# Two conditioning blocks moved late into the first mixer, chunk 9's second token tile made in chunk 10, and fewer unread products

## Chip, cores and metric

One core of one Trainium2 chip runs the kernel. The metric is the device time of one execution in microseconds (us); the median of 3 runs of the kernel before is 1123.04 us (1118.69 to 1125.08).

## What is computed

Two layers over x of 256 tokens by 1024 features. Each layer is three post-normalised sub-layers: a SwiGLU FFN, a block of four token mixers side by side, and a second SwiGLU FFN. Every sub-layer has its own shift, scale and gate, made from one conditioning vector c. Cut to what matters here:

```python
cs = jax.nn.silu(c)
for l in range(DEPTH):                      # 2
    mod = (cs @ ada_w[l] + ada_b[l]).reshape(bn, 3, 3, D_MODEL)
    shift, scale, gate = mod[:, :, 0, None], mod[:, :, 1, None], mod[:, :, 2, None]
    u = x * (1.0 + scale[:, 0]) + shift[:, 0]
    y = _swiglu(u, ffn_w13[l, 0], ffn_w2[l, 0])          # (silu(a) * g) @ w2, D_FF = 2816
    x = _layer_norm(ALPHA * x + 0.5 * gate[:, 0] * y, ln_g[l, 0], ln_b[l, 0])
    u = x * (1.0 + scale[:, 1]) + shift[:, 1]
    y = _hybrid_mixer(u, ...)     # window attention, top-k attention, mLSTM, S5 + GLU, then w_out
    x = _layer_norm(ALPHA * x + gate[:, 1] * y, ln_g[l, 1], ln_b[l, 1])
    u = x * (1.0 + scale[:, 2]) + shift[:, 2]
    y = _swiglu(u, ffn_w13[l, 1], ffn_w2[l, 1])
    x = _layer_norm(ALPHA * x + 0.5 * gate[:, 2] * y, ln_g[l, 2], ln_b[l, 2])
```

## The kernel before, in words

Five engines each run one written-out order of instructions, tied by semaphores. There is no planner: what an engine does next is what stands next in its block.

**FFN.** D_FF is cut into 11 chunks of 256 columns (`CHUNKS`), c = 0 to 10. TensorE (`ffn_chunk`, lines 571 to 618) makes for a chunk the 96 in-products of 256 columns: two tiles `ft`, two halves, eight slices of features, and three products each, because every f32 operand is split into a high and a low fp32r part. Then it makes 24 out-products of 512 columns, in four parts of six: token tile `tt` (0 or 1) by `ft` (0 or 1). They add into banks 0 to 3 of PSUM over all chunks. Tile tt ends in banks 2tt and 2tt+1. In the last chunk the parts come in the order (tt, ft) = (0,0), (0,1), (1,0), (1,1) and each bank raises `y_ready`. ScalarE makes silu (line 1712) and the high parts of the weights (`w_in_high` 1719, `w_out_high` 1727). VectorE multiplies by the gate half and splits h into parts (`ffn_tile`, 1073 to 1083), and makes the low parts of the weights (`w_in_low` 1088, `w_out_low` 1093).

**The conditioning.** `ada_w` is summed on VectorE in blocks of 512 columns: eight multiply-adds of 128x512 for one block (`ada_block`, lines 1007 to 1025) from a 2 MB load. Nearly all blocks stand at the end of an FFN chunk. Block 10 is loaded in two halves into `xn` and `rot_flat` and is summed in chunk 10 of layer 0's first FFN, four steps ahead of each `ffn_tile` (lines 1335 to 1338). Block 11 is loaded into `work_flat` and summed at the start of layer 0's mixer, between the residual and `s5_rotate_in(0)` (line 1428). Both are read only after the mixer, by `ada_sum(10)` and `ada_sum(11)`.

**The sub-layers' ends.** `deepnorm` (1110 to 1168) on VectorE takes banks 0 and 1 (`gated`, `with_x`, `statistics` for both halves, then the variance), then banks 2 and 3 in the same way; after the mixer alone (s == 1) the second tile is done half by half. ScalarE normalises, TensorE turns xn (`turn`, 505 to 520), and ScalarE and VectorE make the next u from it (`evac_uT`). Between these TensorE runs `ada_sum` products and products that nobody reads (`keep_busy`, line 525).

**The mixer.** VectorE's order late in it: logits of A up to `sink_arg` (line 1535); a wait for `g_spread`; the arguments w (1541, 1542); the convolution's last product (1547), after which TensorE can make line 870; scans; line 1559; rotations out, `s5_skip` (1568), `gelu_argument` (1574), `gelu_product` (1580); the products for oT (1633, then 1637 which raises `od_ready`); then `w_in_low` twice for FFN 2 and `deepnorm`. TensorE needs `od_ready` for the third of the four products of bank 0 in line 920.

**The load queue.** SyncE issues every load, in one order, and waits in that order for the buffers. Late in the mixer the order is: the pieces of w_in; `load_last_out` (453); `load_ffn_in` for chunk 0 of FFN 2 (341), which waits for `w_in_used` of the slot that the mixer's piece 4 reads, raised by `chunk_done(4)` (716) on TensorE; then waits for `cols_turned`, `g_spread` and `conv_step`; `load_ln` (356); `load_ffn_out` (349).

## Time and profile before

| | us |
|---|---|
| median of 3 runs | 1123.04 |
| the profiled execution, its own time | 1119.33 |
| its span in the profile | 1117.0 |
| TensorE busy | 1050.7 (94% of the span) |
| VectorE busy | 906.1 (81%) |
| ScalarE busy | 423.3 (38%) |
| mean granted TensorE clock | 0.984 of full speed |

Stages of the profiled span, by the first products of each: FFN 1 of layer 0 from about 35 to 237 us, its mixer to 374, FFN 2 to 573, FFN 1 of layer 1 to 776, its mixer to 906, FFN 2 to 1103. A timeline row reads: start, length, engine, line, operation, output from inputs, shapes, count; in brackets the idle time of the engine before it and what ended it. Matmuls are pipelined, so the length of one is more than its distance to the next.

### The profile page before, as it was taken

The numbers are of one execution on the slowest core, as the hardware profiler recorded it, in microseconds if no ns is written. First come the engines' busy times: TensorE is split into PE (matmuls) and PEld (weight loads), VectorE is DVE, ScalarE is ACT, GpSimd is POOL, SyncE is SP. The second block draws the span as 40 slices with busy tenths as digits, with TensorE's granted clock in tenths as the row PEclk, the third lists the DMA queues.
The fourth block names the chain that finished last, engine by engine and source line by source line (L and its number), as shares of the span: only waits on it lengthen the run. The fifth ranks groups of instructions, "written<-read, shape, count | busy, mean of one in ns | idle before, by whom it ended". The sixth has DMA issues, their size and how long they took to land.

```text
span 1117.0 us, 17050 instructions
## 1 busy us (share of the span) xinstructions
PE 1050.7 (94%) x6899; PEld 916.8 (82%) x6899; DVE 906.1 (81%) x1523; ACT 423.3 (38%) x574; POOL 35.0 (3%) x56
## 2 busy tenths in 40 slices
PE   1899999988999999999999999999999999999994
PEld 1899989976875789999989989998787568999994
DVE  6798999988975898988879998698897588755555
ACT  0445334322372343333333453332336244333331
POOL 1000000003000000000000000000300000000000
PEclk9899999998999999999999999999999999999998
DMA  9889998972351578898965886787225157564540
GB/s 369 283 307 329 345 306 292 323 219 76 94 190 38 189 267 298 304 320 309 328 211 188 303 290 215 269 313 201 108 86 205 50 187 244 174 225 148 193 151 38
DMA packets 184505, 250.84 MB, mean 225 GB/s; under 512 B 25372, under 2 KB 133216, under 8 KB 183404
## 3 DMA queue, kind: packets, MB, share of 16 engines
q1 hardware_dynamic: 184428, 249.76, 65.7%
q8 instruction: 55, 0.90, 0.3%
q14 instruction: 22, 0.18, 0.0%
HBM read 248.69 MB, written 1.05 MB: 224 GB/s over the span
## 4 chain that ended last, share of the span: by engine, by line
PE 73%; DVE 16%; DMA 4%; issue 3%; ACT 3%; SPq 1%; POOL 0%; POOLq 0%; DVEq 0%; ACTq 0%
PE PS L587 11%; PE PS L588 11%; PE PS L586 11%; PE PS L695 8%; PE PS L610 5%; PE PS L614 5%; PE PS L613 5%; DMA w_in_ring<-in_ffn_w_dram 4%; DVE w_in_lo L1088 3%; PE PS L920 2%; PE PS L702 2%; DVE acc L1024 2%; PE PS L780 2%; ACT w_in_hi L1719 2%; PE PS L561 2%
## 5 line engine op out<-in xcount | busy, mean ns | idle before, releaser
L588 PE MATMUL PS<-u_hi,w_in_lo 128*128 128x256 f32 x1280 | 359.9, 281 | 0.0
L587 PE MATMUL PS<-u_lo,w_in_hi 128*128 128x256 f32 x1280 | 359.1, 281 | 0.0
L586 PE MATMUL PS<-u_hi,w_in_hi 128*128 128x256 f32 x1280 | 358.8, 280 | 0.0
L586 PEld LDWEIGHTS PS<-u_hi,w_in_hi 128*128 128x128 f32 x1280 | 241.7, 189 | 1.8
L587 PEld LDWEIGHTS PS<-u_lo,w_in_hi 128*128 128x128 f32 x1280 | 240.4, 188 | 1.6
L588 PEld LDWEIGHTS PS<-u_hi,w_in_lo 128*128 128x128 f32 x1280 | 240.2, 188 | 0.0
L1088 DVE TENSOR_TENSOR w_in_lo<-w_in_ring,w_in_hi 128x2048 fp32r<-128x2048 f32 x88 | 201.2, 2289 | 30.4 <-ACT w_in_hi L1719 30.3
L1719 ACT ACTIVATE w_in_hi<-w_in_ring 128x2048 fp32r<-128x2048 f32 x88 | 168.0, 1914 | 4.1 <-DMA w_in_ring<-in_ffn_w_dram 4.1
L610 PE MATMUL PS<-w_out_hi,h_parts 128*128 128x512 f32 x352 | 145.0, 412 | 11.3 <-DVE h_parts L1082 11.3
L1727 ACT ACTIVATE w_out_hi<-w_out_ring 128x1024 fp32r<-128x1024 f32 x88 | 88.6, 1055 | 152.8 <-PE PS L614 152.8
L1712 ACT ACTIVATE arena<-PS 128x256 f32<-128x256 f32 x88 | 33.8, 384 | 286.5 <-PE PS L588 263.8
L614 PE MATMUL PS<-w_out_hi,h_parts 128*128 128x512 f32 x352 | 138.3, 393 | 0.0
L613 PE MATMUL PS<-w_out_lo,h_parts 128*128 128x512 f32 x352 | 138.1, 392 | 0.0
L1093 DVE TENSOR_TENSOR w_out_lo<-w_out_ring,w_out_hi 128x1024 fp32r<-128x1024 f32 x88 | 103.6, 1219 | 16.3 <-ACT w_out_hi L1727 16.0
L1024 DVE SCALAR_TENSOR_TENSOR acc<-arena,cs,acc 128x512 f32<-128x512 f32 x126 | 94.7, 752 | 4.5
L695 PE MATMUL PS<-uT,w_in_ring 128*128 128x256 f32 (+1 forms) x416 | 96.1, 388 | 1.3 <-issue 1.0
L610 PEld LDWEIGHTS PS<-w_out_hi,h_parts 128*128 128x128 f32 x352 | 66.1, 188 | 33.6 <-issue 20.9
L695 PEld LDWEIGHTS PS<-uT,w_in_ring 128*128 128x128 f32 (+1 forms) x416 | 78.1, 191 | 17.1 <-issue 5.6
L1077 DVE TENSOR_TENSOR arena<-arena,PS 128x256 f32<-128x256 f32 x88 | 36.7, 417 | 68.1 <-ACT arena L1712 67.9
L614 PEld LDWEIGHTS PS<-w_out_hi,h_parts 128*128 128x128 f32 x352 | 66.1, 188 | 15.7
L613 PEld LDWEIGHTS PS<-w_out_lo,h_parts 128*128 128x128 f32 x352 | 66.1, 188 | 15.4 <-issue 2.6
L1082 DVE TENSOR_TENSOR h_parts<-arena,h_parts 128x256 fp32r<-128x256 f32 x88 | 37.4, 425 | 3.0
(305 smaller groups left out, 1183.3 us busy)
## 6 DMA issues: line engine op xcount, KB each, us to landing
w_in_ring<-in_ffn_w_dram SPq DMA_DIRECT2D x88, 1024.0 KB, 7.7
arena<-in_ada_w_dram SPq DMA_DIRECT2D x30, 2048.0 KB, 8.4
w_out_ring<-in_ffn_w_dram SPq DMA_DIRECT2D x44, 1024.0 KB, 6.2
w_in_ring<-in_w_in_dram SPq DMA_DIRECT2D x6, 1024.0 KB, 7.2
w_in_ring<-in_w_in_dram SPq DMA_DIRECT2D x10, 512.0 KB, 5.2
w_out_ring<-in_w_out_dram SPq DMA_DIRECT2D x4, 1024.0 KB, 10.1
w_in_ring<-in_w_in_dram SPq DMA_DIRECT2D x2, 2048.0 KB, 8.7
w_in_ring<-in_w_out_dram SPq DMA_DIRECT2D x4, 1024.0 KB, 5.9
```

The costliest lines, as they stand in the source:

```text
L586: pe.matmul(y, hi, u_hi[:, kt, :], start=(i == 0), stop=False)
L587: pe.matmul(y, hi, u_lo[:, kt, :], start=False, stop=False)
L588: mm = pe.matmul(y, lo[:, kt, half, :], u_hi[:, kt, :], start=False, stop=(i == KT - 1))
L610: mm = pe.matmul(y, h_hi, w_out_hi[ft][:, cols], start=(first and ft == 0), stop=False)
L613: pe.matmul(y, h_hi, w_out_lo[slot][:, ft, cols], start=False, stop=False)
L614: mm = pe.matmul(y, h_lo, w_out_hi[ft][:, cols], start=False, stop=(last and ft == 1))
L695: mm = pe.matmul(o[0:w, :], w_in_ring[(G_MIX + m) % 2][:, kt, c0:c0 + w], uT[:, kt, :], start=(i == 0), stop=(i == KT - 1))
L1024: v.scalar_tensor_tensor(acc[:, :], part(buf, t), cs[:, t:t + 1], acc[:, :], ALU.mult, ALU.add).then_inc(sem("acc_step"), 1)
L1088: v.tensor_tensor(w_in_tile(w_in_lo, slot, ft), w_in_tile(w_in_ring, slot, ft), w_in_hi[ft][:, :, :, :].bitcast(F32), ALU.subtract).then_i ...
L1093: v.tensor_tensor(w_out_lo[slot][:, ft, :], w_out_ring[slot][:, ft, :], w_out_hi[ft][:, :].bitcast(F32), ALU.subtract).then_inc(sem("w_out ...
L1719: a.activation(w_in_hi[ft][:, :, :, :], w_in_tile(w_in_ring, slot, ft), ACT.Copy).then_inc(sem("w_in_high"), 1)
L1727: a.activation(w_out_hi[ft][:, :], w_out_ring[slot][:, ft, :], ACT.Copy).then_inc(sem("w_out_high"), 1)
```

## The change

On VectorE, blocks 10 and 11 are summed as eight pairs of two steps each: pairs 0 to 3 are block 10, pairs 4 to 7 block 11. Each pair has a load of 512 KB, into four buffers used twice (half of `uT_lo`, the two rows of `ln_bc`, half of `rot_flat`). Pairs 0 and 1 stand right after `sink_arg`, pair 2 after `gelu_argument(0)`, 3 after `s5_skip(1)`, 4 and 5 after `gelu_product(1)`, 6 after the oc products, 7 after the od products. From pair 2 on a load waits for the sum of the pair two before it. For layer 0 one `w_in_low` is moved from before the deepnorm after the mixer to after `evac_uT`, and at the end of FFN 2 another is moved in the same way.

In chunk 10 the parts of chunk 9's second token tile come in: the order is (9;1,0), (10;0,0), (10;0,1), (9;1,1), (10;1,0), (10;1,1). Chunk 10 has its own buffers for h and for w_out's high part. `deepnorm` does the second tile half by half after every sub-layer. Two `keep_busy` products go at the start of each mixer and three at the end of FFN 2 of layer 0, where two of four sums move between the turns.

```diff
-ADA = {(0, 0): dict(zip(range(11), range(0, 11))), ...
+ADA = {(0, 0): dict(zip(range(10), range(0, 10))), ...
+        w_out_hi_last = [over(f"w_out_hi_last{ft}", "rot_flat", [P, D], D * ft) for ft in range(2)]
+        h_ring_last = arena[:, 0:512].rearrange("p (s n) -> p s n", n=T)
+        h_parts_last = over("h_parts_last", "arena", [P, 4, T])
+        ada_pairs = [ap.rearrange("p (t n) -> p t n", n=AW) for ap in (
+            uT_lo[:, 4:8, :].rearrange("p a n -> p (a n)"), ln_bc[:, 0, :], ln_bc[:, 1, :], rot_flat[:, 0:2 * AW])]
+            def load_ada_pair(k):
+                n, t = 10 + k // 4, 2 * (k % 4)
+                block = ada_at(n)[1]
+                if k >= 2:
+                    sp.wait_ge(sem("acc_step"), 80 + 2 * (k - 1))
+                    waited(sp)
+                sp.dma_start(ada_pairs[k % 4], ada_w[0, :, block * AW:(block + 1) * AW].rearrange("(p t) n -> p t n", t=8)[:, t:t + 2, :]
+                             ).then_inc(sem(f"ada_pair_loaded{k % 2}"), 16)
...
                     if c in ADA[l, f]:
+                        if l == 1 and f == 0 and c == 0:
+                            sp.wait_ge(sem("y_ready"), 12)
+                            waited(sp)
                         load_ada(ada_w_sb, ADA[l, f][c], "ada_loaded")
-                    if l == 0 and f == 0 and c == 4:
-                        load_ada_half(10, 0)
-                    if l == 0 and f == 0 and c == 9:
-                        sp.wait_ge(sem("rot_step"), ROT_STEPS)
-                        load_ada_half(10, 1)
...
-                if l == 0:
-                    sp.wait_ge(sem("y_ready"), 4)
-                    load_ada(ada_w_2, 11, "ada_2_loaded")
...
                 load_ffn_in(l, 1, slot2, 0, ring_use(l, G_FFN2))
+                if l == 0:
+                    sp.wait_ge(sem("sb_ready"), l + 1)
+                    waited(sp)
+                    load_ada_pair(0)
+                sp.wait_ge(sem("conv_step"), l * 12 + 12)
+                waited(sp)
+                if l == 0:
+                    load_ada_pair(1)
                 sp.wait_ge(sem("cols_turned"), l + 1)
                 waited(sp)
                 sp.wait_ge(sem("g_spread"), l + 1)
                 waited(sp)
-                sp.wait_ge(sem("conv_step"), l * 12 + 12)
-                waited(sp)
+                if l == 0:
+                    load_ada_pair(2)
+                    sp.wait_ge(sem("st_ready"), l + 1)
+                    waited(sp)
+                    load_ada_pair(3)
+                load_ffn_out(l, 1, slot2, 0, out_use(l, out_group(1, 0)))
+                if l == 0:
+                    for k in range(4, 8):
+                        load_ada_pair(k)
+                    sp.wait_ge(sem("acc_step"), 96)
+                    waited(sp)
                 load_ln(l, 1)
-                load_ffn_out(l, 1, slot2, 0, out_use(l, out_group(1, 0)))
...
+                if last:
+                    out_part(c - 1, 1, 0)
+                for tt, ft in ((0, 0), (0, 1)) if c >= CHUNKS - 2 else ((0, 0), (1, 0), (0, 1), (1, 1)):
                     if tt == 0:
                         pe.wait_ge(sem("w_out_split"), tile + (ft + 1))
                         pe.wait_ge(sem("h_done"), tile + (ft + 3))
+                    out_part(c, tt, ft)
+                if last:
+                    out_part(c - 1, 1, 1)
+                    out_part(c, 1, 0)
+                    out_part(c, 1, 1)
...
                     ada_sum(early[i], PS[:, 6, 4 * i:4 * i + 4])
-                    keep_busy(1)
+                keep_busy(1)
...
                     ada_sum(early[i], PS[:, 6, 4 * i:4 * i + 4])
-                    if i == 2:
-                        keep_busy(1)
...
-                    for i, n in enumerate((14, 15, 16, 17)):
+                    for i, n in enumerate((14, 15)):
                         ada_sum(n, PS[:, 6, 4 * i:4 * i + 4])
-                        if i < 3:
-                            keep_busy(1)
-                    turn(xn, l, 2, 1)
+                    keep_busy(1)
+                    def other_sums():
+                        for i, n in enumerate((16, 17)):
+                            ada_sum(n, PS[:, 6, 4 * i + 8:4 * i + 12])
+                    turn(xn, l, 2, 0, other_sums)
                     keep_busy(1)
...
+            def ada_pair(k):
+                t = 2 * (k % 4)
+                ada_block(10 + k // 4, ada_pairs[k % 4], f"ada_pair_loaded{k % 2}", k // 2 + 1, range(t, t + 2), t)
...
                 for tt in range(2):
-                    if s == 1 and tt == 1:
+                    if tt == 1:
...
                 for ft in range(2):
-                    if l == 0:
-                        ada_block(10, None, "ada_halves_loaded", ft + 1, ts=range(4 * ft, 4 * ft + 4))
                     ffn_tile(ft, tile)
...
-                if l == 0:
-                    ada_block(11, ada_w_2, "ada_2_loaded", 1)
                 v.wait_ge(sem("rot_step"), (l + 1) * ROT_STEPS)
...
                 v.tensor_tensor(ds_a, sk, mx_a, ALU.subtract).then_inc(sem("sink_arg"), 1)
+                late_pairs(0, 1)
                 v.wait_ge(sem("g_spread"), l + 1)
...
                 gelu_argument(0)
+                late_pairs(2)
...
                 s5_skip(1)
+                late_pairs(3)
...
                 gelu_product(1)
+                late_pairs(4, 5)
                 v.wait_ge(sem("hn_turned"), l + 1)
...
+                late_pairs(6)
                 for t in range(2):
                     v.wait_ge(sem("glu_tanh"), l * 2 + t + 1)
...
+                late_pairs(7)
-                for ft in range(2):
+                for ft in range(1 + l):
                     w_in_low(G_FFN2 % 2, ft, ff_tile(l, 1, 0) + ft)
...
-                a.wait_ge(sem(f"w_out_used{1 - slot}"), out_use(l, g - 1) + 2)
+                if c == CHUNKS - 1:
+                    a.wait_ge(sem("rot_step"), (l + 1) * ROT_STEPS)
+                else:
+                    a.wait_ge(sem(f"w_out_used{1 - slot}"), out_use(l, g - 1) + 2)
```

## Rows read from the trace of the kernel before

**Rows 1.** The page's busy times and instruction counts of each engine

```profile
PE 1050.7 (94%) x6899; PEld 916.8 (82%) x6899; DVE 906.1 (81%) x1523; ACT 423.3 (38%) x574; POOL 35.0 (3%) x56
```

**Rows 2.** Timeline of TensorE: both mixers' first in-products, their lines 870 and one 780

```profile
246.21 7.14 PE L695 MATMUL PS<-uT,w_in_ring 128*128 128x256 f32 x32 [0.15 <-ACT uT L1688]
...
329.91 1.96 PE L870 MATMUL PS<-rot_flat 64*128 64x256 f32 x16 [2.28 <-DVE rot_flat L1547]
331.80 5.04 PE L780 MATMUL PS<-w_out_ring,uT 128*128 128x512 f32 x8
...
784.85 7.14 PE L695 MATMUL PS<-uT,w_in_ring 128*128 128x256 f32 x32 [0.15 <-ACT uT L1688]
...
862.45 2.02 PE L870 MATMUL PS<-rot_flat 64*128 64x256 f32 x16 [2.27 <-DVE rot_flat L1547]
```

**Rows 3.** Timelines around block 10, chunk 10 of layer 0's first FFN: VectorE, then TensorE

```profile
228.76 3.10 DVE L1024 SCALAR_TENSOR_TENSOR acc<-rot_flat,cs,acc 128x512 f32<-128x512 f32 x4
```

```profile
233.12 0.47 PE L610 MATMUL PS<-w_out_hi,h_parts 128*128 128x512 f32 x1 [2.52 <-DVE h_parts L1082]
```

**Rows 4.** Timeline of SyncE's queue: loads issued late in layer 0's mixer

```profile
323.95 0.99 SPq L341 DMA_DIRECT2D w_in_ring<-in_ffn_w_dram  x2
326.08 1.04 SPq L356 DMA_DIRECT2D ln_bc<-in_ln_g_dram  x1
327.16 0.46 SPq L356 DMA_DIRECT2D ln_bc<-in_ln_b_dram  x1
```

**Rows 5.** Loads of 322 to 338 us: count, KB each, median us to landing

```profile
w_in_ring<-in_ffn_w_dram SPq DMA_DIRECT2D x2, 1024.0 KB, 7.5
ln_bc<-in_ln_g_dram SPq DMA_DIRECT2D x1, 512.0 KB, 8.1
ln_bc<-in_ln_b_dram SPq DMA_DIRECT2D x1, 512.0 KB, 8.5
```

**Rows 6.** The same view, 280 to 400 us: the load of 512 KB alone on the queue

```profile
w_in_ring<-in_w_in_dram SPq DMA_DIRECT2D x1, 512.0 KB, 4.0
```

**Rows 7.** Timeline of VectorE late in layer 0's mixer, where the pairs go

```profile
322.78 0.16 DVE L1535 TENSOR_TENSOR small<-sinks_sb,small 128x8 f32<-128x8 f32 x1
325.94 0.49 DVE L1541 SCALAR_TENSOR_TENSOR work_flat<-PS,small,mask_c 128x256 f32<-128x256 f32 x1 [3.01 <-PE PS L857]
...
350.70 0.47 DVE L1568 SCALAR_TENSOR_TENSOR xn<-uT_lo,prm,PS 128x256 f32<-128x256 f32 x1
...
354.28 0.43 DVE L1580 SCALAR_TENSOR_TENSOR xn<-xn 128x256 f32<-128x256 f32 x1 [0.48 <-ACT xn L1889]
...
360.32 0.79 DVE L1637 SCALAR_TENSOR_TENSOR uT<-xn 128x256 f32<-128x256 f32 x2 [1.42 <-ACT xn L1904]
```

**Rows 8.** Busy us and counts of 38 to 40 us; 0.50 is the granted clock

```profile
38.00:40.00 2.00, 2.00 (x11) 2.00 (x11) 1.95 (x6) 2.00 (x3) 0.00 (x0) 0.50 1.09 349
```

**Rows 9.** Timeline of TensorE: the mixer's last products, layer 0

```profile
359.56 13.90 PE L920 MATMUL PS<-w_in_ring,uT 128*128 128x512 f32 x32
```

**Rows 10.** Timeline of TensorE, last chunk of layer 1's second FFN

```profile
1098.22 0.47 PE L610 MATMUL PS<-w_out_hi,h_parts 128*128 128x512 f32 x1 [0.42 <-DVE h_parts L1082]
...
1102.22 0.40 PE L614 MATMUL PS<-w_out_hi,h_parts 128*128 128x512 f32 x1
```

**Rows 11.** Timelines of VectorE: deepnorms after mixer 0 and FFN 2, chunk 10 of layer 1

```profile
371.00 0.68 DVE L1127 TENSOR_TENSOR xn<-PS,gate_bc 128x512 f32<-128x512 f32 x1
...
375.74 0.21 DVE L1141 BATCH_NORM_AGGREGATE mv<-stats 128x2 f32<-128x12 f32 x1
...
570.98 1.28 DVE L1127 TENSOR_TENSOR xn<-PS,gate_bc 128x512 f32<-128x512 f32 x2
...
574.76 0.21 DVE L1141 BATCH_NORM_AGGREGATE mv<-stats 128x2 f32<-128x12 f32 x1
...
769.12 0.43 DVE L1082 TENSOR_TENSOR h_parts<-arena,h_parts 128x256 fp32r<-128x256 f32 x1
```

**Rows 12.** The line of the unread products: least, median and most ns, first and last

```profile
L525 PE MATMUL PS<-dist,ident x34: 486/487/585, 239.1 to 911.7; 128*128 128x384 f32 x34
```

More of the change, by code:

```diff
@@ L503, in _, with turn @@
             mm.then_inc(sem("consts_turned"), 1)
-            def turn(src, l, s, between=0):
+            def turn(src, l, s, between=0, other=None):
                 if s is not None:
@@ L520, in turn @@
                         keep_busy(between)
+                        if other is not None:
+                            other()
             def keep_busy(count):
@@ L600, in ffn_chunk, with out_part @@
                         spread_gate(n)
-                for k, (tt, ft) in enumerate(((0, 0), (0, 1), (1, 0), (1, 1)) if last else ((0, 0), (1, 0), (0, 1), (1, 1))):
+                def out_part(c, tt, ft):
+                    slot = ff_group(f, c) % 2
+                    parts, his = (h_parts_last, w_out_hi_last) if c == CHUNKS - 1 else (h_parts, w_out_hi)
+                    for hf in range(2):
+                        tok, cols = slice(tt * P, (tt + 1) * P), slice(hf * 512, (hf + 1) * 512)
+                        h_hi, h_lo = parts[:, 2 + ft, tok], parts[:, ft, tok]
+                        y = PS[:, 2 * tt + hf, :]
+                        mm = pe.matmul(y, h_hi, his[ft][:, cols], start=(c == 0 and ft == 0), stop=False)
+                        if (tt, ft, hf) == (0, 0, 0):
+                            mm.then_inc(sem(f"w_in_used{slot}"), 1)
+                        pe.matmul(y, h_hi, w_out_lo[slot][:, ft, cols], start=False, stop=False)
+                        mm = pe.matmul(y, h_lo, his[ft][:, cols], start=False, stop=(c == CHUNKS - 1 and ft == 1))
+                        if c == CHUNKS - 1 and ft == 1:
+                            mm.then_inc(sem("y_ready"), 1)
+                        elif (tt, ft, hf) == (1, 1, 1):
+                            mm.then_inc(sem(f"w_out_used{slot}"), 1)
+                if last:
+                    out_part(c - 1, 1, 0)
+                for tt, ft in ((0, 0), (0, 1)) if c >= CHUNKS - 2 else ((0, 0), (1, 0), (0, 1), (1, 1)):
                     if tt == 0:
@@ L999, in first_mods, with ada_block @@
                                 ).then_inc(sem("mod_step"), 1)
-            def part(buf, t):
-                if buf is not None:
-                    return buf[:, t, :]
-                return ada_halves[t // 4][:, t % 4, :]
-            def ada_block(n, buf, loaded, count, ts=range(8)):
+            def ada_block(n, buf, loaded, count, ts=range(8), first=0):
                 acc = acc_of(n)
@@ L1535, in _, with late_pairs @@
                 v.tensor_tensor(ds_a, sk, mx_a, ALU.subtract).then_inc(sem("sink_arg"), 1)
+                def late_pairs(*ks):
+                    for k in ks if l == 0 else ():
+                        ada_pair(k)
+                late_pairs(0, 1)
                 v.wait_ge(sem("g_spread"), l + 1)
@@ L1649, in _ @@
                 evac_uT(2, l * 24 + 16, l * 3 + 3, l * 2 + 1)
+                if l == 0:
+                    w_in_low(G_FFN2 % 2, 1, ff_tile(l, 1, 0) + 1)
                 for c in range(CHUNKS):
@@ L1657, in _ @@
                     mod_cols(20, 2, 6, 0, SUMMED[21])
-                    w_in_low(0, 0, ff_tile(l + 1, 0, 0))
                 def ffn1_mods():
@@ L1670, in _ @@
                     evac_uT(0, l * 24 + 24, l * 3 + 4, l * 2 + 2)
-                    w_in_low(0, 1, ff_tile(l + 1, 0, 0) + 1)
+                    for ft in range(2):
+                        w_in_low(0, ft, ff_tile(l + 1, 0, 0) + ft)
         @block.scalar
```

46 lines of the change are left out of this document (14 added, 32 removed).

## Prediction

> **What bounds the kernel now.** I read the page first. TensorE is busy for 94% of the span [rows 1], so only three things can move the end: TensorE's own work, the few places where it waits, and its clock. The change takes no product away that anyone reads. I then listed, from TensorE's timeline, the idle times in front of its instructions: beyond the start, only a handful are over 1 us. One is the 2.52 us in chunk 10 of layer 0's first FFN, ended by VectorE's h [rows 3]; one is the 2.28 us before line 870 in each mixer, ended by VectorE's line 1547 [rows 2]. The third view sets the two mixers side by side. From the first in-product to line 870 layer 0 takes 329.91 - 246.21 = 83.70 us and layer 1 takes 862.45 - 784.85 = 77.60 [rows 2]. The work is the same but for block 11 on VectorE, so this difference holds the whole price of block 11, the slow clock after its stall included. The fourth view is the queue of loads, since each pair needs a load of its own.
>
> Everything is worked against the profiled execution (1119.33 us, span 1117.0). The median of the runs is 3.7 us above that, and I add the net to the median. Changes are signed: minus is faster. A difference under 0.5% (5.6 us) can't be told from none.
>
> **Block 11 leaves the mixer's start: -6.1.** VectorE then goes to `s5_rotate_in` as it does in layer 1: 77.60 in place of 83.70 [rows 2].
>
> **The end of FFN 1, layer 0: -4.5.** Consecutive out-products stand (1102.22 - 1098.22)/17 = 0.235 us apart [rows 10], so a part of six is 1.41 us. Two parts leave chunk 9, so chunk 10's in-products start 2.8 us earlier; their weights' low parts and free banks are there by then, made by VectorE in chunk 9. Part (9;1,0) then fills 1.4 us in which TensorE waited for h, and block 10's eight steps of 0.78 us (3.10 for four) no longer stand ahead of h [rows 3]. Before, part (0,1), the one that makes tile 0 final, began at 233.12. Now: in-products end 2.8 earlier, (9;1,0) and (10;0,0) follow, and (10;0,1) begins near 228.0, 5.1 us earlier. From here VectorE's `deepnorm` is the bound: three more parts run before tile 1's last one starts, while tile 0 keeps VectorE for about 4 us. Its second tile is now done half by half. That costs: in this order tile 1 takes 375.74 - 371.00 = 4.74 us, 4.5 without the wait in it; in plain order 574.76 - 570.98 = 3.78, 3.9 with the neg_mean [rows 11]. So 0.6 us is given back: 5.1 - 0.6 = 4.5.
>
> **The other three ends.** At the end of the last FFN, (0,1) began at 1098.22 after a wait of 0.42 [rows 10]. Two parts fewer stand in chunk 9 and one more ahead of it in chunk 10, 1.4 us net, and with (9;1,0) as filling the wait of 0.42 and its 0.2 us of refilling go: it starts 2.0 us earlier, minus 0.6: **-1.4**. At the end of FFN 2, layer 0, deepnorm began only at 570.98, because `w_in_low` stood before it on VectorE [rows 11]. With that moved behind, it begins near 568.2, minus 0.6 = 2.2 earlier. But both `w_in_low` (2.2 us each) now stand between `evac_uT` and the first h of layer 1, where VectorE had 0.95 us of slack; of the 2.2 some 0.8 is lost there: **-1.4**. At the end of FFN 1, layer 1, h of tile 0 ends at 769.12 + 0.43 [rows 11], because VectorE is behind with block 29 and the S5 blocks, not TensorE. Moving parts can't help that: TensorE would stand idle 1.5 us before (10;0,0), and the 0.7 us won is eaten by the 0.6. What is left is TensorE's own queue before the turns, two unread calls shorter: **-0.8**.
>
> **The unread products: nothing of their own.** A call is two records [rows 12] and takes some 0.7 us. They fill time in which TensorE waits for `deepnorm`; only at layer 1's boundary is that queue the bound, counted above. Below nothing they can't be. Above it: the clock may fall where the filling is gone. Gaps of 0.99 us or less at boundaries and the one of 2.52 us [rows 3] were not followed by half speed, 2.28 us in the mixer was, so I take 0 and keep 1.7 us for each boundary as the end of the range.
>
> **The pairs' VectorE time.** Sixteen steps of 0.78 us are 12.5 us. VectorE's gaps late in the mixer, 3.01 before line 1541 and 1.42 before line 1637 [rows 7] with four of 1.4 to 4.1 us between them, would hold them. The loads decide whether they do.
>
> **Pairs 0 and 1: +11.2.** This is the largest term. The load of pair 0 stands behind `load_ffn_in` in SyncE's order, and that waits for the mixer's piece 4: its two loads were issued at 323.95 and took the queue 0.99 us [rows 4]. So pair 0 is issued at about 325, although its buffer is free long before, and 2 MB are ahead of it. Before, the two `load_ln` of 512 KB stood in this place: issued at 326.08 and 327.16 [rows 4], landed 8.1 and 8.5 us later [rows 5], at 334.2 and 335.7. They were 1.4 us apart, the pace of a saturated queue, so an earlier issue won't help: pair 0 lands at 334.2, pair 1 at 335.6. VectorE comes to pair 0 at 322.9 [rows 7] and stands. It sums pair 0 by 335.5 and pair 1 from 335.6 to 337.15. Only then can it take `g_spread` and line 1541, which began at 325.94 [rows 7]: 11.2 us later. Queued behind it are lines 1541 to 1547, and TensorE waits for these at line 870 with nothing else to do. Its 2.28 us of idle become 13.5, at a point where it ran without a gap to the mixer's end. All of it reaches the end. Bounds: at the fastest, if pairs share the queue with the 2 MB rather than follow, 9; at the slowest 12.
>
> **The clock after that idle: +1.0.** After the 2.28 us, line 780 took 5.04 us for eight records that elsewhere take 0.43 each [rows 2, 9]: 1.6 lost at half speed. At the start of the kernel, after 20 us of idle, TensorE was at half (0.50, which is 1.2 GHz) still at 38 to 40 us [rows 8], long after it had work again. Lower bound 0 more than before, upper 3.5; 1.0 is nearer to the row that has the same work behind it.
>
> The Trainium skill (TensorE: Matmul & The Clock Gate, Part 1: The HAM clock gate) says that an idle array falls to half clock and that the ramp depends on the run; by this the term is real but its size differs from run to run. No run here shows that yet.
>
> **Pairs 2 to 7: +1.5.** In the time of before: pair 2 (load long done) and pair 3 (after 350.70 + 0.4) fit gaps. Pair 5's load can go only after pair 3 is summed, 352.8. A load of 512 KB alone took 4.0 [rows 6]; with the larger ones in view I take 4.3. Pair 4 is summed after 354.7 to 356.1, pair 5 from 357.2 to 358.8, the oc products follow by 359.6, still in time for line 920 at 359.56 to 359.7 [rows 9]. Pair 6's load goes after pair 4, at 356.2, lands at 360.6, and is summed by 362.15; the od products (0.79) end at 362.95 in place of 361.1 [rows 7]. TensorE needs them four records of 0.43 after 359.7, at 361.4 [rows 9]: 1.5 idle. Pair 7 ends by 364.7, and one `w_in_low` fits before deepnorm as two did. Bounds 0 (loads in 3 us) and 5.5 (8.1 us each, as behind a full queue).
>
> The Trainium skill (DMA: Bandwidth & Descriptors, Anatomy of one DMA) gives a fixed cost of about 2.0 us and 436 GB/s, by which a pair alone would land in 3.2 us, as an estimate, and this term would be 0.4; the trace's 4.0 for that size says it is more.
>
> **Sum.** -6.1 - 4.5 - 1.4 - 1.4 - 0.8 = -14.2, and 11.2 + 1.0 + 1.5 = +13.7. Net -0.5: the profiled execution would stay at 1118.8, the median at 1122.5.
>
> **Rivals.**
> *No stall at pairs 0 and 1.* The gaps take the pairs as they are placed: 1123.04 - 14.2 + 1.5 = 1110.3. For it speaks only that the placing is made to fit the 3.01 us gap. Against it stands 323.95 in the queue. Between it and the sum lie cases in which the boundaries give more. Chance 0.22 for all that end below by over 5.6 us.
>
> *The clock stays low through the mixer's tail.* Place: from line 870 to line 920, where products are small and sparse after 13.5 us of idle. TensorE is the bound there, so half speed for T us costs T/2, less the 1.6 already paid. It decides from T = 14 on: 1122.5 - 1.0 + 7 - 1.6 = 1126.9 there, and with T = 20, which is nearly to line 920, 1129.9; 1128.6, the 0.5% bound, is at T = 17.4. For it: half speed at 38 to 40 us [rows 8]. Against: dense products brought it back at 41. Chance 0.18, with late pairs in it.
>
> *The ends give nothing.* If VectorE is the bound at every end, as at layer 1's, only block 11 and the 2.5 us in front of h come off: -8.6 + 13.7 = +5.1, 1128.1. Against: in the last FFN it was h made late, after the in-products, for which TensorE waited 0.42 us [rows 10], not a VectorE behind with its work. It counts with "same".
>
> **How the numbers follow.** The sum as worked out, with the third rival, has 0.60; the first 0.22, the second 0.18. Favourable bounds (9, 0, 0) give -5.2, or 1117.8; a part of the first rival is needed for 8 in 10, so the low end is 1114. Unfavourable bounds of the clock and the pairs give 1129.
>
> **What would show it.** In the profile after: the load of pair 0 issued about 1 us behind L341, with some 9 us to landing; VectorE idle some 11 us before the first sum of block 10, ended by a load; TensorE idle 12 to 14 us before line 870 of layer 0 and 2.3 in layer 1; no gap of 2.3 us before line 727; the granted clock at 0.50 around line 870; chunk 10's part (10;0,1) 5 us earlier in layer 0. An idle time under 5 us before line 870 would make the prediction wrong.

## The result, and the profile after

| | before | after |
|---|---|---|
| median | 1121.09 us (20 runs, 1118.61 to 1125.08) | 1125.81 us (20 runs, 1122.74 to 1128.17) |
| profiled execution, its span | 1119.33, 1117.0 | 1126.45, 1123.8 |
| mean granted TensorE clock | 0.984 | 0.972 |

The ratio is 1.0037 with a 95% interval of 1.0026 to 1.0047: the change costs 0.37%, or 4.2 us on the 1123.04 from which the prediction started. That is inside the half per cent that the prediction can't tell from none, and inside its range; but it is a real loss, and the sum had -0.5. Some 4.7 us are to be found.

The page of the changed kernel, its busy times, answers to [rows 1]:

```profile
PE 1052.9 (94%) x6885; PEld 923.1 (82%) x6885; DVE 907.6 (81%) x1523; ACT 422.9 (38%) x574; POOL 35.0 (3%) x56
```

TensorE runs 14 instructions fewer (the seven calls of `keep_busy` whose results nobody reads, two records each: the unread products) and is busy 2.2 us longer. Work cannot have grown, so the clock is the first suspect. The timeline of SyncE's queue, 310 to 330 us (after L347, which is `load_ffn_in`, L325 is `load_ada_pair`), answers to [rows 4]:

```profile
313.81 0.99 SPq L347 DMA_DIRECT2D w_in_ring<-in_ffn_w_dram  x2
314.91 2.97 SPq L325 DMA_DIRECT2D uT_lo<-in_ada_w_dram  x1
317.99 8.91 SPq L325 DMA_DIRECT2D ln_bc<-in_ada_w_dram  x2
```

The loads issued from 305 to 345 us, with KB each and median us to landing, answer to [rows 5, 6]:

```profile
w_in_ring<-in_ffn_w_dram SPq DMA_DIRECT2D x2, 1024.0 KB, 8.3
...
uT_lo<-in_ada_w_dram SPq DMA_DIRECT2D x1, 512.0 KB, 10.2
rot_flat<-in_ada_w_dram SPq DMA_DIRECT2D x1, 512.0 KB, 3.6
```

VectorE's timeline there answers to [rows 7] (L1566 was 1535, L1049 and L1052 are the sums, L1578 was 1541, L1678 was 1637):

```profile
312.64 0.16 DVE L1566 TENSOR_TENSOR small<-sinks_sb,small 128x8 f32<-128x8 f32 x1
325.17 0.49 DVE L1049 TENSOR_SCALAR acc<-uT_lo,cs 128x512 f32<-128x512 f32 x1 [12.37 <-DMA uT_lo<-in_ada_w_dram]
325.69 0.75 DVE L1052 SCALAR_TENSOR_TENSOR acc<-uT_lo,cs,acc 128x512 f32<-128x512 f32 x1
326.91 1.54 DVE L1052 SCALAR_TENSOR_TENSOR acc<-ln_bc,cs,acc 128x512 f32<-128x512 f32 x2 [0.47 <-DVE acc L1052]
328.36 0.48 DVE L1578 SCALAR_TENSOR_TENSOR work_flat<-PS,small,mask_c 128x256 f32<-128x256 f32 x1
...
362.88 1.54 DVE L1052 SCALAR_TENSOR_TENSOR acc<-ln_bc,cs,acc 128x512 f32<-128x512 f32 x2 [0.70 <-DMA ln_bc<-in_ada_w_dram]
364.34 0.75 DVE L1678 SCALAR_TENSOR_TENSOR uT<-xn 128x256 f32<-128x256 f32 x2
```

And TensorE's timeline; the row at 227.59 is the first product of part (10;0,1), 5.5 us earlier than in [rows 3], and the others answer to [rows 2, 3, 9] (L629 was 610, L724 was 695, L899 was 870, L809 was 780, L949 was 920):

```profile
227.59 0.39 PE L629 MATMUL PS<-w_out_hi_last,h_parts_last 128*128 128x512 f32 x1
...
242.22 1.03 PE L724 MATMUL PS<-uT,w_in_ring 128*128 128x256 f32 x4
...
332.33 3.06 PE L899 MATMUL PS<-rot_flat 64*128 64x256 f32 x16 [14.84 <-DVE rot_flat L1584]
...
365.15 12.29 PE L949 MATMUL PS<-w_in_ring,uT 128*128 128x512 f32 x28 [0.43 <-DVE uT L1678]
...
871.79 1.65 PE L899 MATMUL PS<-rot_flat 64*128 64x256 f32 x16 [2.28 <-DVE rot_flat L1584]
```

What the prediction said would show it is there: pair 0's load 1.1 us behind L347, 12.37 us of VectorE's time waiting for it, and 14.84 us of idle TensorE before the old line 870 in layer 0 against 2.28 in layer 1. So I cut both spans at the same products and set the pieces against the sum's terms ("turn" is the transposing of a tile on TensorE; the turn of b_blk is the first work after an FFN that stands ahead of a mixer). The starts come from TensorE's timelines; the last two columns are two kernels of the experiments, for later.

| start of | before | after | i_pairs_again | j_busy_again |
|---|---|---|---|---|
| end of FFN 1, layer 0 (turn of b_blk) | 237.79 | 233.58 | 234.05 | 235.16 |
| mixer, layer 0 | 246.21 | 242.22 | 243.22 | 243.59 |
| line 870 | 329.91 | 332.33 | 321.83 | 321.29 |
| FFN 2, layer 0 | 380.18 | 384.16 | 371.21 | 370.66 |
| its end (sum of block 14) | 573.36 | 577.29 | 564.37 | 563.79 |
| FFN 1, layer 1 | 583.41 | 587.23 | 573.72 | 571.66 |
| its end | 776.42 | 782.47 | 767.92 | 765.87 |
| mixer, layer 1 | 784.85 | 793.55 | 778.09 | 774.29 |
| FFN 2, layer 1 | 912.71 | 920.40 | 906.15 | 902.20 |
| span's end | 1117.0 | 1123.8 | 1109.6 | 1105.6 |

| piece | predicted | after minus before |
|---|---|---|
| up to the mixer of layer 0 | -4.5 | -4.0 |
| its start, up to `load_ffn_in` (323.95 - 246.21 against 313.81 - 242.22) | -6.1 | -6.15 |
| from there to line 870 | +11.2 | +12.56 |
| line 870 to FFN 2 (clock 1.0, late pairs 1.5) | +2.5 | +1.56 |
| FFN 2 of layer 0 with its end | -1.4 | -0.16 |
| FFN 1 of layer 1 with its end | -0.8 | **+4.88** |
| mixer of layer 1 | 0 | -1.01 |
| last FFN | -1.4 | -0.89 |
| sum | -0.5 | +6.8 |

(The two profiled executions differ by more than the medians: that of before was one of its quicker ones.) The stall and block 11 are where they were put, within 1.4 us. Most of the miss is in one piece, FFN 1 of layer 1 with its end: there the two parts of chunk 9, the `w_in_low` ahead of it and the unread products at its ends were moved. The -1.01 of layer 1's mixer is no effect: two executions of one kernel, b and i of the experiments below, take 126.85 and 128.06 us for it. These are TensorE's rows at the end of FFN 1 of layer 1 in the changed kernel, from `ada_sum` (L550) over the unread call (L544) and the turn (L532) to the mixer's first product. The turn of the kernel before stands ahead of them, for comparison:

```profile
782.75 1.94 PE L515 MATMUL PS<-ident,xn 128*128 128x128 f32 x16
```

```profile
782.47 0.63 PE L683 MATMUL PS<-ident,b_blk 128*128 128x128 f32 x4 [0.26 <-issue]
782.93 0.95 PE L550 MATMUL PS<-ones,sig_o 128*128 128x1 f32 x8
783.74 1.03 PE L550 MATMUL PS<-ones,qk_tanh 128*128 128x1 f32 x8
784.64 1.55 PE L544 MATMUL PS<-dist,ident 128*128 128x384 f32 x2
785.98 1.06 PE L697 MATMUL PS<-ident,c_blk 128*128 128x128 f32 x4
786.84 1.70 PE L550 MATMUL PS<-ones,qk_tanh 128*128 128x1 f32 x8
788.40 1.85 PE L550 MATMUL PS<-ones,arena 128*128 128x1 f32 x8
790.11 3.65 PE L532 MATMUL PS<-ident,xn 128*128 128x128 f32 x16
793.55 1.73 PE L724 MATMUL PS<-uT,w_in_ring 128*128 128x256 f32 x4
```

and the windows view at the boundary ahead of that FFN and here, in the changed kernel, and last the kernel before at this end (the stretch, its length, busy us and counts of PE, PEld, DVE, ACT and POOL, then the granted clock):

```profile
586.00:590.00 4.00, 4.00 (x16) 3.35 (x15) 3.77 (x11) 3.87 (x9) 0.00 (x0) 0.50 1.04 392
788.00:792.00 4.00, 4.00 (x20) 4.00 (x21) 0.65 (x5) 1.51 (x2) 0.00 (x0) 0.50 0.68 273
```

```profile
780.00:784.00 4.00, 4.00 (x35) 3.74 (x34) 2.50 (x11) 2.43 (x3) 0.55 (x1) 1.00 1.04 399
```

The granted clock is 0.50, that is 1.2 GHz, although TensorE shows no idle time there: only 0.26 us at 782.47. A sum of the same size took 0.95 at 782.93 and 1.85 at 788.40, the turn 3.65 us where before it took 1.94 for the same 16 products. The boundary takes 11.08 us (782.47 to 793.55) against 8.43 before. At 586 to 590 the low clock runs on 2.8 us into the first in-products of the FFN (587.23 to 590), which should cost half of that, 1.4 us.

### The profile page after: what moved, and what is told of

It is laid out like the page before. It is cut to its first block, busy times and chain, and to the rows that moved or that the text cites. A ratio compares the mean times of both kernels' runs of the same rounds, so it can differ in the third digit from the quotient of the medians.

```text
span 1123.8 us, 17049 instructions
## 1 busy us (share of the span) xinstructions
PE 1052.9 (94%) x6885; PEld 923.1 (82%) x6885; DVE 907.6 (81%) x1523; ACT 422.9 (38%) x574; POOL 35.0 (3%) x56
## 3 DMA queue, kind: packets, MB, share of 16 engines
HBM read 248.69 MB, written 1.05 MB: 222 GB/s over the span
## 4 chain that ended last, share of the span: by engine, by line
PE 70%; DVE 15%; PEld 4%; issue 4%; DMA 3%; ACT 3%; SPq 1%; PEldq 0%; POOL 0%; POOLq 0%; DVEq 0%; ACTq 0%
PE PS L606 11%; PE PS L607 11%; PE PS L605 11%; PE PS L629 6%; PE PS L633 5%; PE PS L632 5%; PE PS L724 5%; DVE w_in_lo L1120 3%; PEld PS L724 3%; PE PS L949 2%; DMA w_in_ring<-in_ffn_w_dram 2%; DVE acc L1052 2%; PE PS L580 2%; ACT w_in_hi L1763 2%; PE PS L581 1%
## 5 line engine op out<-in xcount | busy, mean ns | idle before, releaser
L605 PE MATMUL PS<-u_hi,w_in_hi 128*128 128x256 f32 x1280 | 358.7, 280 | 0.0
L629 PE MATMUL PS<-w_out_hi,h_parts 128*128 128x512 f32 x320 | 132.2, 413 | 8.2 <-DVE h_parts L1114 8.2
L1774 ACT ACTIVATE w_out_hi<-w_out_ring 128x1024 fp32r<-128x1024 f32 x80 | 80.6, 1055 | 137.1 <-PE PS L633 137.1
L633 PE MATMUL PS<-w_out_hi,h_parts 128*128 128x512 f32 x320 | 125.7, 393 | 0.0
L632 PE MATMUL PS<-w_out_lo,h_parts 128*128 128x512 f32 x320 | 125.5, 392 | 0.0
L1125 DVE TENSOR_TENSOR w_out_lo<-w_out_ring,w_out_hi 128x1024 fp32r<-128x1024 f32 x80 | 94.2, 1219 | 14.0 <-ACT w_out_hi L1774 13.9
L1052 DVE SCALAR_TENSOR_TENSOR acc<-arena,cs,acc 128x512 f32<-128x512 f32 x126 | 94.7, 752 | 4.5
L724 PE MATMUL PS<-uT,w_in_ring 128*128 128x256 f32 (+1 forms) x416 | 94.5, 384 | 1.0 <-issue 1.0
L724 PEld LDWEIGHTS PS<-uT,w_in_ring 128*128 128x128 f32 (+1 forms) x416 | 77.4, 189 | 15.4 <-issue 4.5
L629 PEld LDWEIGHTS PS<-w_out_hi,h_parts 128*128 128x128 f32 x320 | 60.1, 188 | 28.6 <-issue 17.1
L633 PEld LDWEIGHTS PS<-w_out_hi,h_parts 128*128 128x128 f32 x320 | 60.1, 188 | 14.2
L632 PEld LDWEIGHTS PS<-w_out_lo,h_parts 128*128 128x128 f32 x320 | 60.1, 188 | 14.1 <-issue 2.6
L580 PE MATMUL PS<-u_hi,w_in_hi 128*128 128x256 f32 x128 | 34.5, 305 | 3.3 <-ACT w_in_hi L1763 2.2
```

Source lines behind the costliest of these rows:

```text
L605: pe.matmul(y, hi, u_hi[:, kt, :], start=(i == 0), stop=False)
L629: mm = pe.matmul(y, h_hi, his[ft][:, cols], start=(c == 0 and ft == 0), stop=False)
L632: pe.matmul(y, h_hi, w_out_lo[slot][:, ft, cols], start=False, stop=False)
L633: mm = pe.matmul(y, h_lo, his[ft][:, cols], start=False, stop=(c == CHUNKS - 1 and ft == 1))
L724: mm = pe.matmul(o[0:w, :], w_in_ring[(G_MIX + m) % 2][:, kt, c0:c0 + w], uT[:, kt, :], start=(i == 0), stop=(i == KT - 1))
L1052: v.scalar_tensor_tensor(acc[:, :], buf[:, t - first, :], cs[:, t:t + 1], acc[:, :], ALU.mult, ALU.add).then_inc(sem("acc_step"), 1)
```

## The experiments

Two theories stood. **Q, the queue's order:** the loss at pairs 0 and 1 is only that their loads stand behind `load_ffn_in` on SyncE. **U, the unread products:** with them the half clock at the boundaries would not be there. Rivals: the pairs' sums themselves cost it on VectorE; and the clock falls by chance, with the unread products or without. From here on the kernels go by the first letters of their labels, and a kernel's boundary is the stretch from the last work of one stage to the first product of the next. Between experiments the numbers are medians with ratios to the kernel before, timed beside it on the same chip.

### Unread products back at all ends (a_busy_back)

```diff
                 for i in range(2):
                     ada_sum(early[i], PS[:, 6, 4 * i:4 * i + 4])
-                keep_busy(1)
+                    keep_busy(1)
...
+                    for i, n in enumerate((14, 15, 16, 17)):
+                        ada_sum(n, PS[:, 6, 4 * i:4 * i + 4])
+                        if i < 3:
+                            keep_busy(1)
+                    turn(xn, l, 2, 1)
```

> The changed kernel with the unread products and the order of the four sums at the ends as they were before. Theory U (the unread products held the clock): no 10 us stretches of granted clock 0.50 after FFN 2 of layer 0 and at the start of layer 1's mixer, and none of 3.4 us at the start of layer 0's mixer; some 8 us less than the changed kernel, about 1118, ratio to before 0.997. Rival (the clock fell there because the stall in the first mixer or the moved parts shifted everything, or by chance): the low stretches stay, time about 1126, ratio 1.004. The stall of 14.8 us before the line of qkT products stays in both.

Measured: 1126.02 us, ratio 1.0038 [1.0025, 1.0052]; nothing gained in sum. U as stated, for all the boundaries, fell. In the trace both mixers did start in 8.42 us, at full clock. But the end of FFN 2 took 13.55 us (576.81 to 590.36) against 9.94 in the changed kernel and 10.05 before: TensorE's queue is longer there, and it ran at half clock all the same.

### Loads of pairs 0 and 1 first (b_pairs_early, i_pairs_again)

```diff
                 slot2 = G_FFN2 % 2
-                load_ffn_in(l, 1, slot2, 0, ring_use(l, G_FFN2))
                 if l == 0:
                     sp.wait_ge(sem("sb_ready"), l + 1)
                     waited(sp)
                     load_ada_pair(0)
                 sp.wait_ge(sem("conv_step"), l * 12 + 12)
                 waited(sp)
                 if l == 0:
                     load_ada_pair(1)
+                load_ffn_in(l, 1, slot2, 0, ring_use(l, G_FFN2))
```

> The changed kernel with the loads of pairs 0 and 1 issued ahead of the load of FFN 2's first weights, everything else as changed. Theory Q (queue order makes the stall): TensorE idles 2.3 us there in place of 14.8, and the slow clock behind it shrinks; 13 us less than the changed kernel, about 1112.5, ratio 0.992. Rival (the pairs' own 3.1 us of VectorE time and later pairs make up for it): less than half of that comes back, ratio about 0.999.

Measured: 1113.20 us, ratio 0.9916 [0.9895, 0.9938]. SyncE's queue, VectorE and TensorE of b_pairs_early at the same place:

```profile
309.06 0.40 SPq L325 DMA_DIRECT2D uT_lo<-in_ada_w_dram  x1
310.84 0.37 SPq L325 DMA_DIRECT2D ln_bc<-in_ada_w_dram  x1
318.35 0.99 SPq L347 DMA_DIRECT2D w_in_ring<-in_ffn_w_dram  x2
```

```profile
317.18 0.16 DVE L1566 TENSOR_TENSOR small<-sinks_sb,small 128x8 f32<-128x8 f32 x1
317.26 0.48 DVE L1049 TENSOR_SCALAR acc<-uT_lo,cs 128x512 f32<-128x512 f32 x1
```

```profile
324.41 1.70 PE L899 MATMUL PS<-rot_flat 64*128 64x256 f32 x16 [2.38 <-DVE rot_flat L1584]
```

VectorE walks from `sink_arg` into pair 0 without a wait, and TensorE's idle time is 2.38 us, as in layer 1. Q holds: the four sums stand in a gap that was there anyway, and the order of three loads is worth 1.0037 - 0.9916 = 0.0121, or 13.6 us, give or take some 3 by the two intervals. The price predicted for the stall and the clock after it was 12.2.

What is left is the rest of the change: 0.9916 is 9.4 us faster than before. By the prediction's terms without the stall it should be -14.2 + 1.5 = -12.7.

### Both edits (c_both)

The two diffs above together.

> Both together: the unread products back and the loads of pairs 0 and 1 early. If U and Q both hold and add, 21 us less than the changed kernel, about 1105, ratio 0.985. If the clock's fall at the ends hangs on the stall, this is no faster than the kernel with early pairs alone, ratio 0.992.

Measured: 1113.30 us, ratio 0.9921 [0.9902, 0.9939]: as b_pairs_early. Again the mixers start in 8.42 us, and the end of FFN 2 takes 13.44, at half clock in the windows view of c_both:

```profile
570.00:574.00 4.00, 4.00 (x18) 3.48 (x17) 0.58 (x4) 0.00 (x0) 0.00 (x0) 0.50 1.07 381
```

So the two edits of a_busy_back, at the mixers and at the end of FFN 2, seem to cancel, and have to be parted.

### The kernel before with only the fewer unread products (d_before_fewer)

In the old kernel: the two `keep_busy` calls off at each mixer's start and three off at the end of FFN 2, and sums 16 and 17 moved between the turns there, as in the change.

> The kernel before with only the unread products removed and the last two of four sums moved between the turns, as in the change. Theory U: stretches of granted clock 0.50 at the ends appear here too, some 8 us more than before, about 1129, ratio 1.007. Rival (the clock's fall needs the rest of the change): ratio 1.000 within 0.2%, perhaps 1 us less.

Measured: 1121.47 us, ratio 1.0002 [0.9986, 1.0018]. No difference in the time, with a mean granted clock of 0.980 against 0.984. The mixers now start in 9.58 and 8.83 us in place of 8.42 and 8.43, and the end of FFN 2 takes 12.14 for 10.05, with a granted clock of 0.50 from 580 to 588. The interval holds 1.8 us either way, so it neither shows nor excludes a price of 2 us.

### The unread products at the mixers alone (e_busy_mixers, j_busy_again)

b_pairs_early with the first half of the first diff: two calls at each mixer's start, nothing at the end of FFN 2.

> Early pairs, the unread products back at the start of both mixers only, the end of FFN 2 as changed. Theory U2 (without them the granted clock falls to half at each mixer's start, with them it doesn't; at FFN 2's end it falls either way): 8.4 us from the end of each FFN 1 to the mixer's first product in both layers, no 0.50 stretch there, 2 to 4 us less than early pairs alone, about 1110.5, ratio 0.990. Rival (they cost on TensorE's queue what they save in clock): no difference to early pairs alone, 1113, ratio 0.992.

Measured: 1108.93 us, ratio 0.9886 [0.9860, 0.9911]. That is 4 us better than b_pairs_early, but the intervals overlap. Both were run again, on one chip.

> The kernel of run b_pairs_early once more, beside that of e_busy_mixers on one chip, since the intervals of those two overlap. The unread products hold the clock (theory): without them a half-clock stretch stands at the start of each mixer, from the end of the FFN to the mixer's first product more than 9 us in at least one layer against 8.4, and the median is 3 to 5 us above that of e: 1113, ratio 0.991. Rival (the clock falls by chance, whether they are there or not): the two agree within 1.5 us.

> The kernel of run e_busy_mixers once more. Theory: 1109, ratio 0.988, both mixer starts 8.4 us at full clock. Rival: within 1.5 us of i_pairs_again.

Measured: i_pairs_again 1112.11, ratio 0.9914 [0.9891, 0.9938]; j_busy_again 1110.18, ratio 0.9899 [0.9874, 0.9923]. Over the 12 executions of each (b and i against e and j, on three chips) the means differ by 2.4 us, with an interval from resampling them of 0.6 to 4.0; i and j alone, on the one chip, give 1.8 (-0.4 to 3.7). The size expected, 3 to 5, is above both; the sign holds, by the pooled runs and by the profiles. The start of layer 0's mixer shows how. First i_pairs_again, without the products (two rows of the windows view, then TensorE's timeline from the last sum but one):

```profile
238.00:242.00 4.00, 4.00 (x23) 4.00 (x23) 1.35 (x7) 2.02 (x3) 0.56 (x1) 0.55 1.02 410
242.00:246.00 4.00, 4.00 (x16) 3.54 (x15) 3.28 (x6) 1.93 (x4) 0.00 (x0) 0.60 0.12 44
```

```profile
237.39 0.95 PE L550 MATMUL PS<-ones,qk_tanh 128*128 128x1 f32 x8
238.20 1.71 PE L550 MATMUL PS<-ones,arena 128*128 128x1 f32 x8
239.77 3.65 PE L532 MATMUL PS<-ident,xn 128*128 128x128 f32 x16
243.22 2.22 PE L724 MATMUL PS<-uT,w_in_ring 128*128 128x256 f32 x5
```

and the same of j_busy_again, with them:

```profile
238.00:242.00 4.00, 4.00 (x31) 3.42 (x31) 2.04 (x8) 2.43 (x3) 0.56 (x1) 1.00 1.05 394
242.00:246.00 4.00, 3.85 (x25) 3.38 (x23) 3.18 (x8) 1.93 (x4) 0.00 (x0) 1.00 0.40 158
```

```profile
239.96 0.89 PE L544 MATMUL PS<-dist,ident 128*128 128x384 f32 x2
240.68 0.95 PE L550 MATMUL PS<-ones,arena 128*128 128x1 f32 x8
241.49 1.94 PE L532 MATMUL PS<-ident,xn 128*128 128x128 f32 x16
243.59 1.75 PE L726 MATMUL PS<-uT,w_in_ring 128*128 128x256 f32 x7 [0.15 <-ACT uT L1734]
```

Without the unread products the turn begins 5.72 us after the turn of b_blk (234.05), with them 6.33 us after (235.16): the queue is 0.6 us shorter. But it takes 3.65 in place of 1.94, and the in-products start at half clock. The start takes 9.17 us against 8.43, and the 4 us from 242 have a clock of 0.60. In layer 1 it is 10.17 against 8.42. In all profiles of kernels with these products (before, a, c, e to h, j to l) both starts took 8.42 or 8.43 us; in all without them (after, b, d, i) both took longer, 8.64 to 11.19. So at the mixers' starts this is no chance. Against c_both (1113.30) e and j are faster too, by 3.0 us in the means (1.1 to 4.7): at the end of FFN 2 the old order, with its three more unread calls, costs in this kernel.

### Chunk 9's parts back in chunk 9 (f_parts_undone, k_undone_again)

```diff
-                if last:
-                    out_part(c - 1, 1, 0)
-                for tt, ft in ((0, 0), (0, 1)) if c >= CHUNKS - 2 else ((0, 0), (1, 0), (0, 1), (1, 1)):
+                for tt, ft in ((0, 0), (0, 1), (1, 0), (1, 1)) if last else ((0, 0), (1, 0), (0, 1), (1, 1)):
...
-                if last:
-                    out_part(c - 1, 1, 1)
-                    out_part(c, 1, 0)
-                    out_part(c, 1, 1)
```

on top of e_busy_mixers.

> The previous kernel (early pairs, unread products at the mixers) with chunk 9's second token tile made in chunk 9 again. The prediction's reckoning (VectorE's deepnorm is the bound at each end): 5 to 6 us more than that kernel. Rival P (TensorE's own queue after the last part is the bound at the mixers' starts, so only its idle time counts): 1 us more at layer 0's mixer, nothing at layer 1's, 2 us more at the kernel's end, 3 us in all, ratio about 0.993.

> The kernel of run f_parts_undone once more: the parts of chunk 9's second token tile back in chunk 9, everything else as in j_busy_again. The prediction's reckoning makes it 4.2 us slower than j (2.8 at FFN 1 of layer 0, 1.4 at the last FFN), 1113; rival, by the timelines of the first such run (the span was shorter, 1105.0): the parts gain where TensorE waited for h and lose about as much in FFN 1 of layer 1, so that it is 0 to 3 us slower.

Measured: 1113.26, ratio 0.9915 [0.9889, 0.9940], and 1111.55, ratio 0.9906 [0.9880, 0.9933]. Over both the mean is 1.7 us above that of e and j (interval -0.2 to 3.5). What either expectation reckoned for the prediction is outside; some gain is likely but not shown by these two alone. The profiles show where it can come from. In FFN 1 of layer 0 the parts bring nothing: from the first in-product of chunk 9 to the last out-product of chunk 10 it takes 35.41 us in f and k, 35.38 or 35.39 in the ten profiles with the parts moved, and 39.05 before, where two waits of 0.78 and 2.52 us for h stood in it. It is block 10's leaving that took these away. In the last FFN the parts bring 1.4: from its first product to the span's end 204.85 and 204.78 in f and k, 203.40 in j.

### The parts undone in FFN 1 of layer 1 alone (l_undone_in_one)

j_busy_again with the old order of parts where l is 1 and f is 0.

> The kernel of j_busy_again with the parts of chunk 9 back in chunk 9 in FFN 1 of layer 1 alone, where VectorE is behind with block 29 and the S5 blocks. If moving them costs there (theory: FFN 1 of layer 1 took 0.7 to 2 us longer with the moved parts), that FFN is 1 us shorter, 1108; the prediction's reckoning (TensorE's idle time there eats what is won) makes no difference, 1109.

Measured: 1109.08, ratio 0.9892 [0.9865, 0.9920]. The mean is 0.7 us below that of j (-3.3 to 2.2), so the time can't tell the two expectations apart. The profiles can. First in-product of chunk 9 and last out-product of chunk 10 in that FFN, in j_busy_again and then in l_undone_in_one:

```profile
730.25 0.28 PE L605 MATMUL PS<-u_hi,w_in_hi 128*128 128x256 f32 x1
...
765.21 0.40 PE L633 MATMUL PS<-w_out_hi_last,h_parts_last 128*128 128x512 f32 x1
```

```profile
733.33 0.28 PE L605 MATMUL PS<-u_hi,w_in_hi 128*128 128x256 f32 x1
...
767.59 0.39 PE L633 MATMUL PS<-w_out_hi_last,h_parts_last 128*128 128x512 f32 x1
```

That is 34.96 us with the parts moved and 34.26 with them in place. All nine profiles with the parts moved there have 34.95 to 34.98, the five others (before, d, f, k, l) 34.24 to 34.27. So moving them costs 0.7 us in this FFN: TensorE waits 0.96 us for h there in place of 0.42. The theory that moving them costs there holds, at the low end of the 0.7 to 2 us that it named; the prediction's reckoning, that it neither helps nor hurts, was 0.7 off.

### The order of deepnorm, and one w_in_low (g_plain_order, h_low_first)

g_plain_order: e_busy_mixers with `deepnorm`'s second tile half by half after the mixer only, as before.

```diff
-                    if tt == 1:
+                    if s == 1 and tt == 1:
...
+                        if tt == 1:
+                            neg_mean(0)
```

> The same kernel (early pairs, unread products at the mixers) with deepnorm's second tile in the plain order after both FFNs. The prediction's reckoning: 0.6 us less at each of four ends, 2.4 us less in all. Rival P: only the kernel's own end, 0.6 us less, which the timing can hardly tell from none, and the distance from the end of FFN 1 to the mixer's first product stays 8.4 us.

Measured: 1108.93, ratio 0.9887 [0.9863, 0.9911], the same as e. h_low_first: one `w_in_low` ahead of the deepnorm at the end of FFN 2 of layer 0 again.

> The same kernel with one low part of weights ahead of the deepnorm at FFN 2's end, as before. The prediction's reckoning: 1.4 us more. Rival (what is won ahead of deepnorm is lost behind evac_uT, because VectorE is behind there with both low parts): no difference, or less by up to 1 us.

Measured: 1109.82, ratio 0.9885 [0.9863, 0.9907], also the same. Neither order shows in the time. At the kernel's own end the plain order is 0.4 us shorter in the profile (203.00 from the last FFN's first product in g, 203.4 in the others with the parts moved). What either order is worth at the end of FFN 2 can't be read, since g and h ran it at half clock (9.72 and 9.44 us) and e at full (7.86). At the mixers' starts it is worth nothing: with the unread products back, the turn follows TensorE's own queue, as 241.49 in the rows of j_busy_again shows, which has no idle time in its bracket.

## Why the prediction missed: the terms that held and the one that failed

**Pairs 0 and 1, +11.2: right, 1.4 short.** 12.56 in the profile; idle TensorE 14.84 where the prediction had 13.5. The landing was reckoned 10.25 us after the issue of `load_ffn_in` (334.2 - 323.95) and came 11.3 after it (314.91 + 10.2 - 313.81). With the clock after it the step was priced at 12.2 and measured 13.6 by b_pairs_early.

**Block 11, -6.1: right**, -6.15 in the profile. **Pairs 2 to 7 and the clock, +2.5:** 1.56; the od products did stand behind pair 6's load (0.70 us in VectorE's row at 362.88), but the price at L949 was 0.43 us of idle time. How much of the 1.56 is clock and how much these waits isn't parted; the same piece takes 49.4 to 51.1 us in the kernels without the stall, 50.27 before. The 3.2 us for a lone load of a pair, which the prediction takes from the Trainium skill (DMA: Bandwidth & Descriptors, Anatomy of one DMA), is that section's fit for loads issued by GpSimd. These are issued by SyncE, and took 4.0 and 3.6.

**The ends, -8.1 together: wrong in detail, and nearly right in sum, in part by luck, once the clock is held.** By the prediction's terms a kernel with the loads in front and the unread products at the mixers has -12.7 + 0.8 = -11.9 us. The two runs of it gave 0.9886 and 0.9899, a mean of -12.1. But the terms behind it are not those of the prediction. It had 2.8 us from the two parts at FFN 1 of layer 0, where the profiles of f and k show nothing; 1.4 in the last FFN, which is there; and 0 in FFN 1 of layer 1, where they cost 0.7. The times give some 1.7 (-0.2 to 3.5) for 4.2. The half-by-half order was to cost 0.6 at each of four ends and costs 0.4 at one; of the moved `w_in_low`, -1.4, nothing shows in the time. That the -4.5 of layer 0 came out at -4.0 is luck in the same way: block 10's leaving took the waits for h from TensorE's queue, and f and k, with the parts in their old places, reach that end at 233.91 and 234.47, among the 233.42 to 235.16 of the kernels with the parts moved. The reasoning "from here VectorE's `deepnorm` is the bound" was wrong at the mixers' starts: the turn came without any idle time in the kernel before too, since the sums and the unread calls ahead of it fill 6.33 us.

**The step that failed: "The unread products: nothing of their own", with the -0.8 that they were to bring at layer 1.** The prediction took gaps as what lowers the clock, looked for idle times at the boundaries, found none over 0.99 us, and chose 0 from a range of 0 to 1.7 for each boundary. There was no gap: the clock fell while TensorE went from one sum of one column to the next. The price by i against j and b against e is +2.4 (0.6 to 4.0), so the step was off by 3.2. With the 1.4 of the stall that is 4.6 of the 4.7 us to be found, but with an uncertainty of some 2 us on the one and 3 on the other, so that the closeness is luck too. In the kernel before the same removal cost nothing that the time shows (d_before_fewer, within 1.8 us).

In the profiled pair more of it shows: FFN 1 of layer 1 with its end took +4.88 where -0.8 was reckoned. 2.65 of it are the half clock at the mixer's start. The other 2.23 are in the FFN itself. 1.47 are in its first chunk, 19.87 us against 18.40, where the clock was low until 590; j_busy_again, at full clock there, has 18.87, so about 1.0 is clock, and the 0.47 that is left goes with waits for h, 1.05 and 0.31 us where before has one of 0.99. And 0.74 are in chunks 9 and 10: the moved parts. A comparison of the whole FFN hides this. In l_undone_in_one, with the parts in their old places, it took 194.4 us against 194.2 in j, because its first chunk took 19.73 us at half clock:

```profile
572.00:576.00 4.00, 4.00 (x16) 3.34 (x15) 3.39 (x10) 3.74 (x9) 0.00 (x0) 0.50 1.03 391
```

What lowers the clock at the end of FFN 2 stays open. It was low there in the changed kernel, but also with the unread products and the sums back in their old places (a, c), and in the old kernel with them taken away (d). Only before had the full clock there by the old order; with the new order j had it throughout, and e lost it at 572. In time that end is better as changed: 9.94 us with the low clock, 7.87 in j_busy_again without, against 10.05 before.

The rivals: "no stall" is what b_pairs_early makes of it, 1110.3 reckoned and 0.9915 x 1123.04 = 1113.5 measured. "The clock stays low through the mixer's tail" did not come: the windows view of the changed kernel has the clock back 6 us after line 870's start, and the tail cost 1.56:

```profile
334.00:338.00 4.00, 4.00 (x12) 2.45 (x12) 3.19 (x5) 3.49 (x9) 0.00 (x0) 0.55 0.33 78
338.00:342.00 4.00, 4.00 (x38) 1.60 (x38) 0.00 (x0) 0.00 (x0) 0.00 (x0) 1.00 0.14 53
```
"The ends give nothing", 1128.1, lies nearer to the result than the forecast, but not for its reason: without the stall it would have e and j 7.1 us faster than before (8.6 less 1.5), and they are 12.1 faster. The ends do give.

## What to carry to other kernels

Before work is moved into a gap of an engine, look at where its load stands in the queue that issues in order: a load whose buffer is free long before can still be late behind one that waits for something else. Products that nobody reads are not free to take away because they are hidden; ask what the engine does without them in that stretch, and read the granted clock there after each change. Where several small gains are added, test the sum in one kernel that holds the disturbing part still. And before two kernels' times for a stage are compared, compare the granted clock in it: l_undone_in_one seemed to show that the moved parts cost nothing, until its slow first chunk was set apart.

## What the runs showed of the hardware

**Half clock without idle time.** In i_pairs_again TensorE is busy for 4.00 of 4.00 us from 238 to 242, mostly with one-column sums and 128-column turns, and the granted clock is 0.55; with two calls of 384 columns more between them it stays at 1.00. The Trainium skill (TensorE: Matmul & The Clock Gate, HAM oscillation — how this bites in real kernels) tells of a clock that falls in waits for transfers; these rows show it low while products follow each other without idle time. The Trainium skill (TensorE: Matmul & The Clock Gate, Part 1: The HAM clock gate) says that the ramp at a kernel's start differs from run to run. What the profiles here show is near to it, but in mid-kernel: at the end of FFN 2 and after it the same kernel has different clocks in different executions. It took 9.38 us in f and 10.94 in k, which is f's kernel; and from 572 to 576 us the granted clock was 0.60 in e and 1.00 in j, which is e's.

**A load's place decides its time.** Loads of 512 KB took 10.2 us to landing behind 2 MB, and 3.6 with no other in flight (pair 3, issued at 335.56). In the changed kernel its issue held SyncE's queue for 2.97 us, in b_pairs_early for 0.40.
